# Attention softmax over two key halves: the second half exponentiated against the common maximum, one correction factor left

## The reference, cut to what matters

```
s = jnp.einsum('bqkgd,bskd->bkgqs', qi, k).astype(jnp.float32) * scale
p = jax.nn.softmax(s, axis=-1).astype(v.dtype)
return jnp.einsum('bkgqs,bskd->bqkgd', p, v)
```

## Time and profile before

| | |
|---|---|
| median of 3 runs | 4936.14 us |
| lowest, highest | 4927.88, 4944.38 us |
| the profiled execution | 4955.78 us, its span 4954.1 us |
| mean granted TensorE clock | 0.931 of full speed |
| attention `sa` | about 290 to 1037 us of the span |
| attention `pa` | after it, to about 1160 us |

### The profile page before, as it was taken

The page is one execution under the profiler, slowest core; times in us unless marked ns, Lnnn a source line. Parts: engine busy times, 40 slices in busy tenths (PEclk is TensorE's granted clock), DMA queues, the critical chain, the costliest instruction groups (busy, mean ns, idle before and its releaser), DMA issues. The chain is left out here.

```text
span 4954.1 us, 142712 instructions
## 1 busy us (share of the span) xinstructions
PE 4263.9 (86%) x61165; PEld 3942.2 (80%) x61166; DVE 3031.0 (61%) x5716; ACT 2036.9 (41%) x3616; POOL 1150.6 (23%) x951
## 2 busy tenths in 40 slices
PE   6979999986888867777777777992799999999998
PEld 5868888865888866667776775772799999999998
DVE  6879999954888874444444445767545444444443
ACT  4568888854555531111111112220344444444443
POOL 4533333321333320100100212320121211211110
PEclk9989999977999979998999988995899999999999
DMA  9910000004333331122112115650465655655654
GB/s 168 184 46 22 24 21 22 24 27 126 129 128 131 131 136 55 55 62 60 55 55 67 55 56 158 203 157 3 158 182 166 178 177 170 183 168 175 177 170 109
DMA packets 519591, 542.01 MB, mean 109 GB/s; under 512 B 75200, under 2 KB 456384, under 8 KB 519104
## 3 DMA queue, kind: packets, MB, share of 16 engines
q1 hardware_dynamic: 411840, 425.00, 27.2%
q10 hardware_dynamic: 92480, 62.93, 5.7%
q0 software_dynamic: 14784, 46.57, 4.5%
HBM read 377.99 MB, written 156.43 MB: 108 GB/s over the span
## 5 line engine op out<-in xcount | busy, mean ns | idle before, releaser
L2287 DVE TENSOR_TENSOR g_wlo<-g_raw,g_whi 128x2048 fp32r<-128x2048 f32 x192 | 439.3, 2288 | 115.4 <-ACT g_whi L2249 115.4
L2249 ACT ACTIVATE g_whi<-g_raw 128x2048 fp32r<-128x2048 f32 x192 | 366.4, 1909 | 145.2 <-DMA g_raw<-expert_w_gate 145.2
L2358 PE MATMUL g_pD<-g_whi,g_hh 128*128 128x256 f32 x1536 | 417.6, 285 | 2.5 <-ACT g_o L2276 2.4
L2358 PE MATMUL g_pD<-g_wlo,g_hh 128*128 128x256 f32 x1536 | 408.4, 279 | 0.0
L517 POOL TENSOR_SCALAR saprob<-saprob,sarate 128x1024 f32<-128x1024 f32 x256 | 283.7, 1121 | 458.6 <-DVE sarate L597 458.6
L1107 PE MATMUL c_pP<-c_xh,c_whi 128*128 128x258 f32 x1120 | 335.8, 300 | 46.8 <-DMA c_gup<-g_lora_up 28.3
L540 ACT ACTIVATE saph<-sapT 128x512 fp32r<-128x512 f32 x512 | 291.5, 596 | 125.8 <-PE sapT L636 125.6
L1372 DVE TENSOR_TENSOR d_pm<-d_pP,d_fixed 128x128 f32<-128x128 f32 x400 | 114.3, 289 | 365.1 <-PE d_pP L1429 364.6
L1259 POOL TENSOR_TENSOR d_kr<-d_kr,d_fixed 128x512 f32<-128x512 f32 x80 | 103.1, 1293 | 1009.2 <-ACT d_kr L1293 1009.0
L581 DVE TENSOR_TENSOR sapl<-sapT,saph 128x512 fp32r<-128x512 f32 x512 | 329.1, 685 | 2.5 <-ACT saph L540 2.5
L571 DVE TENSOR_REDUCE sanm<-sapS 128x1 f32<-128x1024 f32 x256 | 312.7, 1221 | 26.1 <-PE sapS L624 16.3
(11 more groups left out here) (361 smaller groups left out, 14236.7 us busy)
## 6 DMA issues: line engine op xcount, KB each, us to landing
g_raw<-expert_w_gate SPq DMA_DIRECT2D x64, 1024.0 KB, 5.6
g_raw<-expert_w_up SPq DMA_DIRECT2D x64, 1024.0 KB, 5.5
g_raw<-expert_w_down SPq DMA_DIRECT2D x64, 1024.0 KB, 5.2
ops<-c_ops SPq DMA_DIRECT2D x40, 1024.0 KB, 4.0
d_bd<-ops SPq DMA_DIRECT2D x80, 512.0 KB, 3.9
c_xh<-xT_hi SPq DMA_DIRECT2D x10, 1032.0 KB, 5.6
c_xl<-xT_lo SPq DMA_DIRECT2D x10, 1032.0 KB, 8.6
x_in<-x SPq DMA_DIRECT2D x20, 512.0 KB, 8.1
```

The lines of the kernel that those rows point to most:

```text
L2249: act.activation(w_hi[:, Q % NBUF, :, :], raw[:, Q % NRAW, :, :], ACT.Copy).then_inc(s["g_hi"], 1)
L2287: dve.tensor_tensor(w_lo[:, Q % NBUF, :, :], raw[:, Q % NRAW, :, :], w_hi[:, Q % NBUF, :, :].bitcast(F32), ALU.subtract).then_inc(s["g_lo" ...
L2358: mm = pe.matmul(pD[k][:, 0:WB], x[:, d, k * P:(k + 1) * P], w[:, b, d, :], start=(d == 0 and i == 0), stop=(d == DC - 1 and i == len(part ...
```

## The change

Unit 1 is now exponentiated against the common minimum `nmin` in place of its own, so its exponential waits for `common`, and its share is 1. One share per head is left, that of unit 0. `total` becomes one fused multiply and add (sum0 x share + sum1) and a reciprocal, which is `rate`, now one column for both units. GpSimd multiplies unit 0 by `rate` and by `share` in one instruction with two per-row scalars, and unit 1 by `rate` and 1.0. Since GpSimd now reads `share`, ScalarE waits before it overwrites a share until GpSimd has done unit 0 of head h-2. For `pa` (NU = 1) nothing changes.

```diff
@@ gpsimd
-                        pool.tensor_scalar(prob[:, h % 4, keys], prob[:, h % 4, keys], rate[:, h % 2, u:u + 1], 1.0, ALU.mult, ALU.mult).then_inc(s["norm"], 1)
+                        to_common = share[:, h % 2:h % 2 + 1] if u < NU - 1 else 1.0
+                        pool.tensor_scalar(prob[:, h % 4, keys], prob[:, h % 4, keys], rate[:, h % 2:h % 2 + 1], to_common, ALU.mult, ALU.mult).then_inc(s["norm"], 1)
@@ scalar, exps
-                    act.wait_ge(s["nm"], NU * head(t, h) + u + 1)
-                    act.activation(prob[:, h % 4, u * UW:(u + 1) * UW], pS[u][:].rearrange("p k n -> p (k n)"), ACT.Exp, bias=nm[:, h % 2, u:u + 1],
+                    if u == 0:
+                        act.wait_ge(s["nm"], NU * head(t, h) + 1)
+                    else:
+                        act.wait_ge(s["nmin"], head(t, h) + 1)
+                    act.activation(prob[:, h % 4, u * UW:(u + 1) * UW], pS[u][:].rearrange("p k n -> p (k n)"), ACT.Exp,
+                                   bias=nm[:, h % 2, 0:1] if u == 0 else nmin[:, h % 2:h % 2 + 1],
                                    scale=-1.0, accum_out=den[:, h % 2, u:u + 1]).then_inc(s["exp"], 1)
@@ scalar, shares
-                    act.activation(share[:, h % 2, :], nm[:, h % 2, :], ACT.Exp, bias=nmin[:, h % 2:h % 2 + 1], scale=-1.0).then_inc(s["share"], 1)
+                    tb, hb = back(t, h, 2)
+                    if live(tb):
+                        act.wait_ge(s["norm"], NU * head(tb, hb) + 1)
+                    act.activation(share[:, h % 2:h % 2 + 1], nm[:, h % 2, 0:1], ACT.Exp, bias=nmin[:, h % 2:h % 2 + 1], scale=-1.0).then_inc(s["share"], 1)
@@ vector, total
-                    dve.tensor_tensor(part[:, h % 2, :], den[:, h % 2, :], share[:, h % 2, :], ALU.mult).then_inc(s["part"], 1)
-                    dve.wait_ge(s["part"], head(t, h) + 1)
-                    dve.tensor_reduce(dsum[:, h % 2:h % 2 + 1], part[:, h % 2, :], AX.X, ALU.add).then_inc(s["ds"], 1)
+                    k = slice(h % 2, h % 2 + 1)
+                    dve.scalar_tensor_tensor(out=dsum[:, k], in0=den[:, h % 2, 0:1], scalar=share[:, k], in1=den[:, h % 2, 1:2],
+                                             op0=ALU.mult, op1=ALU.add).then_inc(s["ds"], 1)
                     dve.wait_ge(s["ds"], head(t, h) + 1)
-                    dve.reciprocal(rden[:, h % 2:h % 2 + 1], dsum[:, h % 2:h % 2 + 1]).then_inc(s["rd"], 1)
-                    dve.wait_ge(s["rd"], head(t, h) + 1)
-                    dve.tensor_scalar(rate[:, h % 2, :], share[:, h % 2, :], rden[:, h % 2:h % 2 + 1], None, ALU.mult).then_inc(s["rate"], 1)
+                    dve.reciprocal(rate[:, k], dsum[:, k]).then_inc(s["rate"], 1)
```

More of the change, by code:

```diff
@@ L449, in attention @@
         nmin = sb(name + "nmin", [P, 2])
-        share = sb(name + "share", [P, 2, NU])
-        part = sb(name + "part", [P, 2, NU])
+        share = sb(name + "share", [P, 2])
         prob = sb(name + "prob", [P, 4, nk])
@@ L454, in attention @@
         dsum = sb(name + "dsum", [P, 2])
-        rden = sb(name + "rden", [P, 2])
-        rate = sb(name + "rate", [P, 2, NU])
+        rate = sb(name + "rate", [P, 2])
         ph = sb(name + "ph", [P, 2, n_tiles, 2, P], F32R)
@@ L462, in attention @@
         pO = [ps(f"{name}pO{k}") for k in range(2)]
-        s = sems("id q0 q1 score nm nmin exp share part ds rd rate norm tr hi lo pv osb st0 st1 seen", name + "_")
+        s = sems("id q0 q1 score nm nmin exp share ds rate norm tr hi lo pv osb st0 st1 seen", name + "_")
         block = ctx.enter_context(nc.Block())
@@ L587, in total @@
                     if NU == 1:
-                        dve.reciprocal(rate[:, h % 2, :], den[:, h % 2, :]).then_inc(s["rate"], 1)
+                        dve.reciprocal(rate[:, h % 2:h % 2 + 1], den[:, h % 2, :]).then_inc(s["rate"], 1)
                         return
                     dve.wait_ge(s["share"], head(t, h) + 1)
-                    dve.tensor_tensor(part[:, h % 2, :], den[:, h % 2, :], share[:, h % 2, :], ALU.mult).then_inc(s["part"], 1)
-                    dve.wait_ge(s["part"], head(t, h) + 1)
-                    dve.tensor_reduce(dsum[:, h % 2:h % 2 + 1], part[:, h % 2, :], AX.X, ALU.add).then_inc(s["ds"], 1)
+                    k = slice(h % 2, h % 2 + 1)
+                    dve.scalar_tensor_tensor(out=dsum[:, k], in0=den[:, h % 2, 0:1], scalar=share[:, k], in1=den[:, h % 2, 1:2],
+                                             op0=ALU.mult, op1=ALU.add).then_inc(s["ds"], 1)
                     dve.wait_ge(s["ds"], head(t, h) + 1)
-                    dve.reciprocal(rden[:, h % 2:h % 2 + 1], dsum[:, h % 2:h % 2 + 1]).then_inc(s["rd"], 1)
-                    dve.wait_ge(s["rd"], head(t, h) + 1)
-                    dve.tensor_scalar(rate[:, h % 2, :], share[:, h % 2, :], rden[:, h % 2:h % 2 + 1], None, ALU.mult).then_inc(s["rate"], 1)
+                    dve.reciprocal(rate[:, k], dsum[:, k]).then_inc(s["rate"], 1)
             def step(t, h):
```

## The result

The changed kernel takes 4896.36 us (median of 7 runs) against 4932.51 us for the kernel before, measured anew beside it. The ratio is 0.9924, with a 95% interval of 0.9899 to 0.9948. By the ratio 37 us are saved, between 26 and 50; the medians lie 36 apart. The forecast was 32.5 us saved.

What follows compares the result with a forecast made beforehand. A loop through VectorE and TensorE, 5.77 us a step, was taken as the bound. With TensorE next at 5.52, 120 steps x 0.25 plus 2.5 us saved 32.5: from 4936.1 to 4904, range 4888 to 4931.

Steps and rivals of the forecast that it cites:

- TensorE took over as the bound: Attention of the long request: TensorE sets the step at 5.52 us, 0.25 of 0.36 us cashed; 68 in 100.
- `total`: VectorE's small instructions between minimum and low parts shrink from 0.71 to 0.35 us, 0.36 us off the loop per step.
- a semaphore cost nothing extra: Skill's rule for VectorE: only 0.20 us a step saved, 25 us, 4911; a version of the 12-in-100 VectorE-bound rival.
- TensorE's free step: TensorE's step in attention of the long request without any wait: 2 x (0.93 + 1.83) = 5.52 us.
- a step below 5.45: Sign of the larger-gain rival: TensorE's pitch hides waits for VectorE, step down to 5.41, 46 us, 4890; 8 in 100.
- VectorE would wait for scores: VectorE by itself needs 5.24 us a step, so about 0.28 a step becomes its wait for TensorE's scores.
- ScalarE's new wait: Unit 1's exponential waits for `common`, 0.12 to 0.27 us late in the old timetable, covered by 0.44 us idle.
- GpSimd: Its two-scalar multiplication of unit 0 takes 1.11 to 2.35 us, with 3.5 us of room; either bound costs nothing.
- The rival that ends slower: GpSimd's two-scalar instruction above 4.66 us sets the step; at 5.0, 43 us slower, 4979; port lock possible; 5 in 100.

Runs made afterwards that it cites:

- padded kernel: Changed kernel with two chained, unused small sums in VectorE's `total`, bringing it back to 0.72 us; ratio 0.9982 to the kernel before, 5.791 us a step.
- 64-byte kernel: Changed kernel with two unused tiles that move `rate` and the high and low parts 64 bytes up, no instruction changed; 5.528 us a step.
- kernel without `total`: Changed kernel without the fused sum and reciprocal in the long request, probabilities left unnormalized; ratio 0.9914 to the kernel before.
- The wait alone: Kernel before, with unit 1's exponential waiting for the common minimum but still using its own; ratio 1.0001, 5.761 us a step.
- moving the product alone: Kernel before, with VectorE's product of reciprocal and shares moved to GpSimd, both units keeping their own minimum; ratio 0.9963.
- fillers: Changed kernel with unread identity transposes on TensorE in the first tile of the short request's attention; 4915.34 us, ratio 0.9880 to the kernel before.

## Why the prediction was right, step by step

The mechanism came as forecast: TensorE took over as the bound, and part of what VectorE lost was cashed. The part that the changed instructions brought is 33 us of the stage, against 32.5 in the forecast. Another 7 us came from the new places of tiles, which the prediction did not have; that they helped and did not harm was luck, and they lie within the uncertainty of the time (26 to 50 us saved).

- **`total`**: forecast 0.71 to 0.35. Measured 0.35, with the fused instruction at 0.21 (forecast 0.22 from two widths) and the spacings 0.24 and 0.11. If a semaphore cost nothing extra, as the Trainium skill has it ("VectorE: DVE Perf Modes", "The DRAIN you can't avoid"), 0.20 would have been saved in place of 0.36; `total` did lose 0.36, so the trace does not agree.
- **TensorE's free step**: forecast 5.52, read from single rows of the halves that did not wait. Over the stage these halves average 2.753 us in the kernel before, which makes 5.51; measured 5.450, or 5.453 by the half steps. This is the one term that was off, 0.25 a step cashed in the forecast against 0.31. At the old places the instructions would give 5.767 - 2 x 2.753 = 0.26 a step, 33 us, and the two small sums of the padded kernel cost as much. The remaining 0.05 a step, 7 us of the 39.7, goes to the places. The 64-byte kernel is not the place of before in full: its `prob` tile lies 32 bytes lower, and its half steps are 2.767. The kernel before with its tiles in the new places was not run, so the 7 us are reckoned and not measured by themselves.
- **Nothing below TensorE's pace**: the measured step stands at the edge of "a step below 5.45", the sign named for hidden waits on VectorE. The kernel without `total`, at 5.445, rules these out.
- **VectorE would wait for scores, 0.2 to 0.3 a step**: by the starts it waits less. Its low parts end at 603.65 and the minimum starts at 603.72, 0.07 after them, where back-to-back ones start about 0.06 before the end (606.51 and 606.45): 0.13. Besides the faster TensorE, VectorE's own sum was 0.08 too low: 1.15 + 0.35 + 1.23 + 1.26 + 0.10 + 1.23 = 5.32 in the step shown, forecast 5.24.
- **ScalarE's new wait**: forecast 0.12 to 0.27 late in the old timetable, covered. The wait alone made it 0.11 late and changed nothing. In the changed kernel a wait of the exponential for `nmin` is listed twice, both times while the pipeline fills.
- **GpSimd**: two scalars cost 1.20 in place of 1.12, inside the bounds. The room was real: 1.25 us more cost nothing. The rival that ends slower has its mechanism, the lock included, but begins at far more work than the change brings.
- **Two halves of the change**: moving the product alone takes 0.228 a step and leaves a wait of 0.04. The common maximum and the fused sum take away that wait, about 5 us in the stage; the rest of the 0.15 by which they shorten `total` is VectorE's time, which TensorE no longer waits for.

What stays open: the gain in time of the moved product (18 us, up to 25; 23 like with like) is less than its 29 us in the stage. The length of the recurrence differs by 6 us between the profiles on that chip, but the runs that were only timed have no trace to show which stage made the difference.

## What to carry to other kernels

When two engines are both nearly full, lay out one step in time and add up the loop that runs through both, then each engine alone; the gain of a cut ends where the next sum begins. Read the next engine's free pace from the places where it did not wait, as a mean over the stage, and allow a per cent or so for tiles that the edit moves (1.4% at most here). An engine that a list of waits no longer names may still wait: compare the halves of its step. Before crediting part of a change, run it with the same tiles in the same places.

## What the runs showed of the hardware beyond that

- Moving the operands of matmuls (and the tiles beside them) by 32 and 64 bytes, with no instruction changed, made the step 5.476 and 5.528 in place of 5.450. The scores' matmuls, whose own operands did not move, went from 390 to 396 ns on average. The mechanism isn't known.
- A VectorE instruction with two SBUF inputs took 0.573 us in place of 0.21 when GpSimd was running, and ended with GpSimd's.
- One stage with the same instructions ran at either level of TensorE's clock in different executions: 106 us at 0.50 and 82 at mostly 1.00. TensorE waits 6.5 us for the first queries just ahead of it. Of the thirteen profiles without fillers (the kernel before included) seven took 106 us, four 82, and two lay between (89 and 98). What decides it in an execution is open.
